# Two weight slots per transfer: a ring of four single slots becomes a ring of two double ones

## The reference, cut to what matters

```
h = rmsnorm(x);  proj = h @ w_in                      # 1024 -> 3584
a_out = s5_branch(...)        # complex diagonal scan, gelu, gate with w_glu (512 x 512)
b_out = rglru_branch(...)     # causal conv of width 4, gates, linear scan
merged = sigmoid(g_a) * (a_out @ w_proj_a) + sigmoid(g_b) * (b_out @ w_proj_b)
x = x + merged @ w_out                                # 1024 x 1024
q = rmsnorm(x) @ w_q                                  # 1024 -> 2048, 8 heads x 2 x 128
# per token and head: the 16 best of 128 x 128 product keys -> 16 experts of 16384
x = x + sum over 8 x 16 experts of  g * gelu(u[e] . h) * v[e]     # rows u[e], v[e] of 1024
y = rmsnorm(x)
```

## Time and profile before

| | |
|---|---|
| median of 3 runs | 3368.29 us (3363.19 to 3371.45) |
| profiled execution, its own time | 3370.61 us |
| its span | 3368.7 us |
| granted TensorE clock, mean | 0.921 of full speed |
| busy PE / DVE / POOL / ACT | 81% / 75% / 37% / 33% of the span |
| moved by DMA | 1240.71 MB, mean 368 GB/s |

### The profile page before, as it was taken

The page is one execution under the profiler, slowest core; times in us unless marked ns, Lnnn a source line. Parts: engine busy times, 40 slices in busy tenths (PEclk is TensorE's granted clock), DMA queues, the critical chain, the costliest instruction groups (busy, mean ns, idle before and its releaser), DMA issues.

```text
span 3368.7 us, 34176 instructions
## 1 busy us (share of the span) xinstructions
PE 2721.4 (81%) x8808; PEld 1530.2 (45%) x8808; DVE 2532.8 (75%) x5859; ACT 1108.4 (33%) x3074; POOL 1235.6 (37%) x1048
## 2 busy tenths in 40 slices
PE   7986888888869888888868888889888996576566
PEld 6855445555435445555434545556534442122122
DVE  6827886887678886778668888787667888666764
ACT  2212433443134432544123442443223433222223
POOL 0001443334343344334343444333344343444443
PEclk9998999999989999999989999999999999788779
DMA  4255999989999999989999999999899998999998
GB/s 131 82 165 197 402 398 419 378 342 393 418 418 376 413 413 394 380 346 387 419 417 386 401 417 409 385 369 365 354 409 387 418 403 321 410 419 410 421 421 340
DMA packets 205499, 1240.71 MB, mean 368 GB/s; under 512 B 27608, under 2 KB 36184, under 8 KB 73200
## 3 DMA queue, kind: packets, MB, share of 16 engines
q0 software_dynamic: 148608, 1082.20, 79.2%
q1 hardware_dynamic: 54176, 147.73, 11.9%
q10 hardware_dynamic: 2512, 8.52, 0.7%
HBM read 1233.81 MB, written 4.55 MB: 368 GB/s over the span
## 4 chain that ended last, share of the span: by engine, by line
DMA 34%; PE 30%; DVE 19%; issue 7%; ACT 4%; DVEq 3%; POOL 2%; ACTq 1%; POOLq 0%
DMA arena<-in_uv,arena 33%; PE psum L1449 15%; PE psum L1385 9%; DVE arena L1216 8%; DVE arena L822 4%; DVE arena L830 3%; ACT arena L585 3%; PE psum L1539 2%; POOL arena L544 2%; PE psum L1396 1%; PE psum L1417 1%; PE psum L1528 1%; ACT L585 1%; ACTq L601 1%; DVE arena L1068 1%
## 5 line engine op out<-in xcount | busy, mean ns | idle before, releaser
L1449 PE MATMUL psum<-arena 128*128 128x512 f32 x3072 | 1595.7, 664 | 562.7 <-ACT arena L585 515.6
L544 POOL DMA_INDIRECT arena<-in_uv,arena x1032 | 1231.6, 1193 | 2105.7 <-PE psum L1449 1321.6
L1216 DVE CUSTOM_DVE_ANT_0 arena<-arena 128x1024 f32<-128x1024 f32 x1024 | 1229.0, 1223 | 543.9 <-DMA arena<-in_uv,arena 520.8
L1449 PEld LDWEIGHTS psum<-arena 128*128 128x128 f32 x3072 | 609.4, 208 | 1415.8 <-ACT arena L585 736.5
L585 ACT ACTIVATE arena<-arena 128x1 f32<-128x1 f32 (+5 forms) x2451 | 689.4, 312 | 1600.1 <-DVE arena L1216 1384.5
L1385 PE MATMUL psum<-arena 128*128 128x256 f32 (+1 forms) x2944 | 686.6, 388 | 15.4 <-DVE arena L830 6.2
L1385 PEld LDWEIGHTS psum<-arena 128*128 128x128 f32 x2944 | 562.1, 193 | 151.6 <-issue 56.3
L830 DVE SCALAR_TENSOR_TENSOR arena<-arena 128x1024 f32<-128x1024 f32 (+4 forms) x451 | 410.2, 916 | 41.8 <-issue 22.9
L822 DVE TENSOR_TENSOR arena<-arena 128x256 f32<-128x256 f32 (+10 forms) x879 | 305.2, 386 | 37.0 <-ACT arena L585 5.8
L585 ACT ACTIVATE arena<-psum 128x256 f32<-128x256 f32 (+6 forms) x261 | 106.4, 419 | 586.0 <-PE psum L1385 573.2
L585 ACT ACT_TABLE_LOAD x222 | 284.8, 1283 | 10.5 <-PE psum L1385 4.0
(11 more groups left out here) (85 smaller groups left out, 836.8 us busy)
## 6 DMA issues: line engine op xcount, KB each, us to landing
arena<-in_w_in SPq DMA_DIRECT2D x112, 512.0 KB, 7.6
arena<-in_w_q SPq DMA_DIRECT2D x64, 512.0 KB, 11.0
arena<-in_uv,arena POOLq DMA_INDIRECT x1032, 11.4
arena<-in_w_ab SPq DMA_DIRECT2D x32, 512.0 KB, 8.2
arena<-in_w_out SPq DMA_DIRECT2D x32, 512.0 KB, 8.0
arena<-in_w_glu SPq DMA_DIRECT2D x16, 256.0 KB, 6.8
arena<-in_x_tok SPq DMA_DIRECT2D x8, 512.0 KB
arena<-in_keys SPq DMA_DIRECT2D x32, 128.0 KB, 7.7
```

The lines of the kernel that those rows point to most:

```text
L544: pool.indirect_dma_start(uvring[:, r], None, i_["uv"], bass.IndirectOffsetOnAxis(column, 0)).then_inc(uv_in[r], 16)
L1216: V.tensor_tensor_reduce(out=u, in0=u, in1=hn[i // (SLOT // 2)], scale=1.0, scalar=0.0, op0=ALU.mult, op1=ALU.add, accum_out=dots_[:, b % ...
L1449: ins = mm(PV[:, half], dg[:, PAIR * (b % 2) + k], uvring[:, i % UV, at:at + 512], start=(i % (SLOT // 2) == 0), stop=(pe_slots(i + 1) == ...
```

## The change

SP loads two neighbouring slots with one transfer. The ring has two places of 8 KB a partition (`RING = 2`, `T.take(RING, 2 * D)`), in the same space as before. On the host, `pairs` lays two slots side by side, so that a row in HBM is 8 KB (4 KB for `w_glu`); what PE reads and computes is the same. A pair is loaded when PE has finished the second slot of the pair two before it: slots `l` and `l + 1` wait for slot `l - 3`, where before slot `l` waited for `l - 4` and slot `l + 1` for `l - 3`. PE waits on the pair's semaphore, for both slots.

```diff
-RING = 4
+RING = 2
-        ring = T.take(RING, D)
+        ring = T.take(RING, 2 * D)
-            weights = [i_["w_in"][m] for m in range(28)] + [i_["w_glu"][m] for m in range(4)] \
-                + [i_["w_ab"][m] for m in range(8)] + [i_["w_out"][m] for m in range(8)] \
-                + [i_["w_q"][m] for m in range(16)]
-            def load_weights(l):
-                width = weights[l].shape[1]
-                sp.dma_start(ring[:, l % RING, 0:width], weights[l]).then_inc(slot_in[l % RING], 16)
+            weights = [i_["w_in"][m] for m in range(14)] + [i_["w_glu"][m] for m in range(2)] \
+                + [i_["w_ab"][m] for m in range(4)] + [i_["w_out"][m] for m in range(4)] \
+                + [i_["w_q"][m] for m in range(8)]
+            def load_weights(p):
+                width = weights[p].shape[1]
+                sp.dma_start(ring[:, p % RING, 0:width], weights[p]).then_inc(slot_in[p % RING], 16)
...
-                for l in range(RING, SLOTS):
+                for l in range(2 * RING, SLOTS, 2):
...
-                    if l >= 48 and l % 2 == 0:
+                    if l >= 48:
...
-                    sp.wait_ge(unit, UNITS * c + slot_unit(l - RING) + 1)
-                    load_weights(l)
+                    sp.wait_ge(unit, UNITS * c + slot_unit(l + 1 - 2 * RING) + 1)
+                    load_weights(l // 2)
...
-                    for l in range(RING):
-                        sp.wait_ge(unit, UNITS * c + slot_unit(SLOTS - RING + l) + 1)
-                        load_weights(l)
+                    for p in range(RING):
+                        sp.wait_ge(unit, UNITS * c + slot_unit(SLOTS - 2 * RING + 2 * p + 1) + 1)
+                        load_weights(p)
...
             def slot(c, l):
-                pe.wait_ge(slot_in[l % RING], 16 * (SLOTS // RING * c + l // RING + 1))
-                return ring[:, l % RING, :]
+                p, at = l // 2, l % 2 * (DB if 28 <= l < 32 else D)
+                pe.wait_ge(slot_in[p % RING], 16 * (SLOTS // 2 // RING * c + p // RING + 1))
+                return ring[:, p % RING, at:at + D]
...
+    def pairs(w):
+        m, p, k = w.shape
+        return w.reshape(m // 2, 2, p, k).transpose(0, 2, 1, 3).reshape(m // 2, p, 2 * k)
```

More of the change, by code:

```diff
@@ L1626 @@
     ins = {
-        "xT": chans(x), "x_tok": x, "w_in": w_in[order], "w_glu": tiles(a["s5_w_glu"][0]),
-        "w_ab": np.concatenate([tiles(a["w_proj_a"][0]), tiles(a["w_proj_b"][0])], axis=2),
-        "w_out": a["w_out"][0].reshape(KT, P, D),
+        "xT": chans(x), "x_tok": x, "w_in": pairs(w_in[order]), "w_glu": pairs(tiles(a["s5_w_glu"][0])),
+        "w_ab": pairs(np.concatenate([tiles(a["w_proj_a"][0]), tiles(a["w_proj_b"][0])], axis=2)),
+        "w_out": pairs(a["w_out"][0].reshape(KT, P, D)),
         "lam_re": states(a["s5_lam_re"][0]), "lam_im": states(a["s5_lam_im"][0]),
@@ L1637 @@
         "lru_bd": bd,
-        "w_q": tiles(a["peer_w_q"][0]),
+        "w_q": pairs(tiles(a["peer_w_q"][0])),
         "keys": a["peer_keys"][0].reshape(2 * HEADS, NKEY, P).transpose(2, 0, 1),
```

## The result

The changed kernel takes 3379.32 us (median of 18 runs, 3369.42 to 3386.56), the kernel before 3367.36 us (18 runs, 3356.55 to 3374.0). The ratio is 1.0036, with a 95% interval of 1.0026 to 1.0045: slower by 12 us. On another chip it was 1.0029 (1.0016 to 1.0042). The forecast was 6 us faster; 3379 lies inside the stated range, but on the other side.

A forecast was written before the change was run, and what follows sets the result against it. It took DMA engines, filled largely by gathers, to bound most stages, and PE and DVE the S5 stage. Saved packets -6.7 us and later loads +1 made about -6 us, 3362 us against the median, range 3340 to 3388.

The forecast's parts named there:

- Two regimes: Stages with full DMA engines, where removed DMA time can count, and the S5 stage, where PE and DVE set the pace.
- Fewer packets: On the weight loads' queue 18432 packets go at 17.3 ns each, removing 19.9 us of all sixteen engines.
- How much of it reaches the end: Outside chunk 0 and the S5 stage 11.2 us are left; 60% of it, 6.7 us, was taken as gain.
- Later loads, slot 32: Even slots, asked for one unit later, might make PE wait at slot 32: 1 us in all, bounds 0 and 9.
- Bursts: In the S5 stage a pair's longer push before gathers could cost 0 to 1.2 us a pair; taken as 0.
- The bursts decide, slower: S5 stage of chunks 1 to 3: 24 pairs at 1.2 us cost 29 us, net +23, 3391 us; chance 0.18.
- Queue turns: DMA engines serve queues in turn by packet, so larger weight packets take a larger share; speaks against the change, counted as nothing.
- Whole DMA time: Rival: DMA alone sets the pace and weights reach the gathers' rate, 24 us go, 3344 us; chance 0.22.
- nothing: Rival: SP's queue cuts the 8 KB rows, or PE and DVE hide freed DMA time: -1 us, 3367; chance 0.14.
- fixed part: Rival: each weight landing's fixed 2.1 us counts, 128 fewer give 275 us, about 3090 us; chance 0.01.

The follow-up runs named there:

- e1: Kernel before, single 512 KB loads in 4 KB rows, but the even slot's load held back so both of a pair leave together: ratio 1.0014 to before.
- e3: Against the kernel before: pairs in 8 KB rows everywhere except slots 12 to 27 (S5), which load singly as before: ratio 1.0011.
- e6: Kernel before with single loads, every slot in 2 KB rows instead of 4 KB (w_glu has them already): ratio 1.0036 to before.
- e7: Against the kernel before: pairs in 8 KB rows only for slots 48 to 63 (w_q), others single: ratio 1.0006.
- e13: Against the kernel before: pairs in 8 KB rows only for slots 0 to 11 and 28 to 47, others single: ratio 0.9995.
- e18: Changed kernel's 1 MB pairs on all slots, but in 4 KB rows, run on another chip: ratio 1.0030 to the kernel before.
- e2: Changed kernel with its 1 MB pairs and ring, but in rows of 4 KB instead of 8 KB: ratio 1.0015 to the kernel before.
- e4: Against the kernel before: pairs in 8 KB rows only in slots 12 to 27 (S5), all others single: ratio 1.0028.
- e16: The changed kernel, unedited, run again on another chip: ratio 1.0029 to the kernel before.

## Why the prediction was wrong, point by point

- **Two regimes.** Held for the loss: the three S5 stages are 19.5 us longer. The 6 GB/s more in the full stretch don't show a gain there, as e1 has 5 more without saving a packet.
- **Fewer packets.** 18432 and 0.6 points of q1's share: held.
- **How much of it reaches the end, "6.7 us".** This step failed, as these 6.7 us did not come. They were to come from the 24 pairs a chunk outside S5. e3 pairs just these slots and is 3.7 us slower (0.7 to 7.1). The price is not what was wrong: 6.7 us for 3 x 24 x 144 = 10368 packets are 10.3 ns each, and e6 measured 8.4 for packets added, which would leave 5.4 us. Why the saving doesn't appear (e7 and e13, its parts, are 2.0 slower and 1.7 faster, both with 0 inside) stays open; bursts in these stages may eat it.
- **Later loads, slot 32.** 0 and 1.4 us in two traces where I took 1: about right. With 1 MB in 4 KB rows, which lands later, PE waits 2.8 to 4.5 us for `w_ab` (e18, e2).
- **Bursts: "I take 0".** This step failed, and it made most of the error. I argued from DVE waiting only 6 times in the S5 stage that gathers had slack there. First, that row covers 168 us of one stage; over the three stages DVE already waited for gathers 40 times, 56.9 us. Second, that a consumer seldom waits doesn't say how much later its input may come. Pairs there cost 9.4 us (e4), 0.39 us for each of 24, and in the changed kernel DVE waits for gathers 73.9 us in these stages.
- **The rival.** "The bursts decide, slower", chance 0.18, named the place, the count and the mechanism. It gave 1.2 us to each pair as exposed, +29, where a third of it was measured, and it took off the 6 us that did not come. The measured parts make 9.4 (e4) + 3.7 (e3) = 13.1 us, against 12.1 and 9.8 for the whole. That 3379 lies inside the stated range is no merit of the forecast, which was faster; the range was wide enough for a part of this rival.
- **Queue turns.** The Trainium skill (DMA: Bandwidth & Descriptors, Queues, rings and completion order) has each engine serve its queues in turn, a whole packet at a time, and such a packet is typically a bundle of some 9 to 17 descriptors (orders to move one piece each). What the profile calls a packet is one row. Here the turns fit single rows, by the 9.0 against 11.8 us and by about one gather row for each weight row; the taking of turns agrees, its unit, as far as these traces tell, doesn't. I read the rule, and then let the row of DVE's few waits overrule it.
- **Whole DMA time, nothing, fixed part.** None came as forecast. The fixed part of a landing is worth nothing as long as nobody waits for a weight load. The 2.0 us that the prediction cites from the Trainium skill (DMA: Bandwidth & Descriptors, Anatomy of one DMA) are given there for transfers issued by GpSimd, while the 2.1 us are of loads issued by SP.

## What to carry to other kernels

A prefetch that nobody waits for should move gently. Merging its transfers saves packets, but sends them as bursts in long turns, and in this kernel the stream on the short ring of buffers paid for that. If a landing gets faster and no one was waiting for it, ask who gave up the engine time, and read that consumer's waits over whole stages, not in one window. Try such a merge by stage: here it cost 9.4 us where the chain behind the gathers is tight, and elsewhere showed no clear gain. Before a sum of one trace is believed, look how far it scatters among kernels in which that part is unchanged.

## What the runs showed of the hardware

- 1 MB beside gathers of 8 KB rows lands in 9.0 us (median) in rows of 8 KB (e16) and in 11.8 us in rows of 4 KB (e18). Two queues take turns on an engine about row for row: 231 to 268 gather rows beside 256 weight rows, 117 to 155 beside 128.
- 23040 more packets of SP's queue beside the gathers, from rows of 2 KB instead of 4 KB, changed the end by 8.4 ns / 16 each, about as much as the 9.1 ns / 16 by which the queue's busy time rose.
- Two 512 KB loads that leave together instead of one unit apart lengthened the kernel by 5 us (e1), with the same bytes, rows and packets.
